# Hymba block on one core: unit-matrix transposes in TensorE's first waits, a transfer counted in two halves, one rounding step moved

## The chip, the core and the metric

The kernel runs on one core of a Trainium2 chip. The core has a matrix engine (TensorE, in the profile PE, with its weight loads as PEld), a vector engine (VectorE, DVE), a scalar engine (ScalarE, ACT), GpSimd (POOL) and a queue processor (SyncE, SP) that only issues transfers here. Each engine works through its own instructions in program order, and the engines wait for each other on semaphores. The metric is the device time of one execution in microseconds, as the median over several executions.

## What is computed

One layer of a transformer-like block on x of 512 tokens by 2048 columns, all in float32:

```python
mod = (silu(c) @ w_ada + b_ada)            # six rows of 2048: shift, scale and gate for each sub-layer
shift_m, scale_m, gate_m, shift_f, scale_f, gate_f = split(mod, 6)
h = rmsnorm(x, g_pre_mix) * (1.0 + scale_m) + shift_m
y = token_mixer(h, w_in, ...)              # h @ w_in, attention and gated linear attention heads, @ w_out
x = x + gate_m * rmsnorm(y, g_post_mix)
h = rmsnorm(x, g_pre_mlp) * (1.0 + scale_f) + shift_f
y = square(relu(h @ w_mlp_in)) @ w_mlp_out
x = x + gate_f * rmsnorm(y, g_post_mlp)
```

The change lies in the first stage alone: the normalised x, the row `scale_m`, and the first columns of `h @ w_in`.

## The kernel before

Every engine has one hand-written program, so the order of work on each engine is the order of its code.

The first stage runs like this. ACT squares and sums the four 128-token blocks of x, POOL forms the inverse roots, and DVE and ACT scale two blocks each (`scale_x`). TensorE then transposes x, 16 column tiles k of four 128x128 transposes each, into six PSUM banks in turn, and ACT copies each tile out (`xn_t`). One transpose is a matmul instruction against the unit matrix `ident`.

Beside this DVE works on `scale_m`. The 2048 by 2048 piece of `w_ada` comes in 16 items `am_item` of four 128x512 slabs, four items to a block of 512 columns, and each item comes as two transfers of two slabs. `add_am(n)` multiplies the slabs of item n by the column of silu(c) and adds them into `am_acc` and `am_odd`; at a block's end the two are added. `sum_columns(block)` on TensorE then sums over the partitions with four matmuls against a column of ones, and `mod_columns(block)` on DVE turns that into the scale `mod_a` of four tiles k and raises `am_col`. `add_am` of the next block stands behind this in DVE's program.

With the scale of block 0 known, ACT forms `in_tmp` for k = 0 to 3 (`fill_operand`), and TensorE begins the "fill": the narrow gate columns (`wm_raw`) and the query columns (`fill_w`) of `h @ w_in`, four tiles k to a block. Half of the fill is done in plain float32 (even units u), half with operands split into a high and a low part (units 1, 3, 5, 7), three matmuls for one product (`split_mm`). For these, ACT rounds the weights (`fill_w_hi`, tile `fill_hi`) and the operand (`fill_x_hi`), and DVE forms the low parts (`fill_weights_lo` and `fill_pair_lo`). DVE's program around the first block, unchanged by the diff except inside `add_am`:

```python
add_items(0, 4)
mod_columns(0)
fill_weights_lo(1)      # waits for ACT's fill_hi of unit 1
add_items(4, 6)
fill_pair_lo(1)
add_items(6, 8)
mod_columns(1)          # waits for TensorE's sum_columns(1)
```

TensorE's program for the fill calls `sum_columns(1)` inside unit 1, ahead of its tile k = 3, so TensorE can't go past this place before DVE has finished `add_items(6, 8)`.

Semaphores named in the change: `am_in[3]` counts the transfers of slot 3, `out_done` those of the output at the very end.

Of the kernel before, what the change touches and what calls it, by code (L numbers as in the profile page):

```python
# [41 lines left out]
P = 128  # L42
# [3 lines left out]
def build_block(nc, x, c, w_ada, b_ada, g_pre_mix, g_post_mix, w_in, b_fgate, w_gla_a2, b_gla_a2,  # L46
                g_fox_out, g_gla_out, w_out, g_pre_mlp, g_post_mlp, w_mlp_in, w_mlp_out, out):
    _, SEQ, D = x.shape
    KT = D // P
    TB = SEQ // P  # L50
# [63 lines left out]
    with ExitStack() as ctx:  # L114
# [95 lines left out]
        def small(name, shape, dt=F32):  # L210
            t = at(name, shape, k_at[0], dt)
            size = 4
            for n in shape[1:]:
                size *= n
            k_at[0] += (size + 31) // 32 * 32
            return t

        ident = small("ident", [P, P])
# [34 lines left out]
        BA, BB = bank[6], bank[7]  # L253
# [6 lines left out]
        def sem(name):  # L260
            return ctx.enter_context(nc.semaphore(name))
# [8 lines left out]
        am_in = [sem(f"am_in{s}") for s in range(4)]  # L270
# [7 lines left out]
        out_done = sem("out_done")  # L278
# [182 lines left out]
        def hid_arrived(o):  # L461
            q = hid_at[o]
            return hop_in[q], 32 * (hid_uses[q].index(o) + 1)
# [23 lines left out]
        PIECES += [(slice(0, SEQ), k) for k in range(KT // 2, KT)]  # L487
        N_PIECES, SECOND, N_SECOND = len(PIECES), KT // 2, KT

        def items_used(n):  # L490
            return AM_BLOCK * (n // 4) + 4 * (n % 4)

# [2 lines left out]
        def gates_read(block):  # L495
            return 3 * block + 1

        def fill_read(u):
            return gates_read(u // 2) + 1 + u % 2 if u < MM_G - 1 else FILL_TILE + GLA_HEADS - 1

        FILL_TILE = gates_read(S_BLOCKS - 1) + 2
        gg_hi_done, GG_HI = fill_halves, 3 * len(SPLIT_UNITS) + 1
        gg_lo_done, GG_LO = fill_w_lo, len(SPLIT_UNITS) + 1
        ada_split, ADA_SPLIT = fill_x_lo, 2 * len(SPLIT_UNITS) + GLA_HEADS
# [23 lines left out]
        block = ctx.enter_context(nc.Block())  # L528
# [3 lines left out]
        def _(sp):  # L532
# [111 lines left out]
            def load_am(n):  # L644
                if n >= 4:
                    sp.wait_ge(am_used, items_used(n - 3))
                block, i = divmod(n, 4)
                col = (SCALE_M, SHIFT_M)[block // S_BLOCKS] + block % S_BLOCKS * 512
                for half in range(2):
                    k = 4 * i + 2 * half  # L650
                    sp.dma_start(am_item[n % 4][:, 2 * half:2 * half + 2, :], w_ada_t[:, k:k + 2, col:col + 512])\
                        .then_inc(am_in[n % 4], 16)

            def load_x(t):
                sp.dma_start(x_raw[:, t, :], x_t[:, t, :]).then_inc(x_in[t], 16)
# [12 lines left out]
            for block in range(S_BLOCKS):  # L668
                for n in range(4 * block, 4 * block + 4):
                    load_am(n)  # L670
                load_wm(block)
                for u in (2 * block, 2 * block + 1):
                    load_fill(u)
# [3 lines left out]
            for n in range(16, 32):  # L677
                load_am(n)
                for mm in FOX_AFTER.get(n, ()):
                    load_fox(0, mm, wait=mm > 1)  # L680
# [83 lines left out]
            for u in range(UNITS):  # L764
                n = 7 * u
# [44 lines left out]
            for half in range(2):  # L810
                sp.wait_ge(o_ready, 3 + half)
                sp.dma_start(out_t[:, 1, half * D // 2:(half + 1) * D // 2], v_raw[raw_at[UNITS][ROLE_OF_T[1]]][:, half, :])\
                    .then_inc(out_done, 16)
            sp.wait_ge(out_done, 16 * (TB + 1))


        @block.tensor
        def _(pe):
# [172 lines left out]
            pe.wait_ge(rows_in, 16 * 9)  # L991
            pe.transpose(bank[5][:, 0:6 * KT], rows_a[:, :], ident[0:6 * KT, 0:6 * KT])
            pe.transpose(bank[5][:, 128:148], rows_b[:, :], ident[0:20, 0:20]).then_inc(rows_steps, 1)
            for k in range(KT):
                if k == 0:
                    pe.wait_ge(xn_ready, TB)
                    pe.wait_ge(rows_steps, COLS_READY)
                if k >= TILES:
                    pe.wait_ge(xt_act, k - TILES + 1)
                for t in range(TB):  # L1000
                    last = pe.transpose(bank[k % TILES][:, t * P:t * P + P], x_raw[:, t, k * P:k * P + P], ident[:, :])
                last.then_inc(x_tr, 1)

            def sum_columns(block):
                pe.wait_ge(am_used, items_used(4 * block + 4))
                if block:
                    pe.wait_ge(am_col, block)
                for j in range(4):
                    col = block // S_BLOCKS * 4 + j
                    last = pe.matmul(BA[:, col:col + 1], am_acc[block % 3][:, j * P:j * P + P], ones[:, 0:1],  # L1010
                                     start=True, stop=True)
                last.then_inc(am_sum, 1)

            sum_columns(0)
            pe.wait_ge(xt_act, KT)
            FILL_SUMS = {3: 1, 7: 2, 11: 3, 14: S_BLOCKS}

# [190 lines left out]
            for i, (n, h) in enumerate(halves):  # L1208
                u, p = n // 7, n % 7
                _, dc, group = unit_at[u]  # L1210
                first = u == 0 or unit_at[u - 1][2] != group
                o = 7 * group + p
# [5 lines left out]
                if u and first and h == 0:  # L1218
                    done, count = hid_arrived(o)
# [44 lines left out]
        def _(act):  # L1264
# [150 lines left out]
            def fill_operand(k):  # L1415
                act.wait_ge(am_col, k // 4 + 1)
                act.activation(in_tmp[:, k, :], xn_t[:, k, :], ACT.Copy, scale=mod_a[:, k:k + 1]).then_inc(fill_tmp, 1)
# [14 lines left out]
            def park(h):  # L1432
                act.wait_ge(fill_used, FILL_TILE + h)
                act.activation(gg[:, h * 512:h * 512 + 512], bank[h][:, :], ACT.Copy).then_inc(fill_park, 1)

            def fill_w_hi(u):
                i = SPLIT_UNITS.index(u)
                act.wait_ge(fill_in[u // 2], 64)
                if i > 1:
                    act.wait_ge(fill_used, fill_read(SPLIT_UNITS[i - 2]))  # L1440
                act.activation(fill_hi[i % 2][:, :, :, :], fill_w[u][:, :, :, :], ACT.Copy).then_inc(fill_halves, 1)

            def fill_x_hi(k):
                act.wait_ge(fill_tmp, k + 1)
                act.activation(in_hi[:, k, :], in_tmp[:, k, :], ACT.Copy).then_inc(fill_halves, 1)

            for block in range(S_BLOCKS):
                units = [u for u in SPLIT_UNITS if u // 2 == block]
                fill_w_hi(units[0])
                for k in range(4 * block, 4 * block + 4):  # L1450
                    fill_operand(k)
                for u in units:
                    if u != units[0]:
                        fill_w_hi(u)
                    fill_x_hi(2 * u)
                    fill_x_hi(2 * u + 1)
# [252 lines left out]
            t, cg, done, count = SQUARES[-1]  # L1709
# [34 lines left out]
        def _(dve):  # L1744
# [272 lines left out]
            def add_am(n):  # L2017
                block, i = divmod(n, 4)
                total = am_acc[block % 3]
                dve.wait_ge(am_in[n % 4], 32 * (n // 4 + 1))  # L2020
                if i == 0 and block >= 3:
                    dve.wait_ge(am_sum, block - 2)
                for j in range(4):
                    part = (total, am_odd)[j % 2][:, :]
                    item, c_k = am_item[n % 4][:, j, :], c_act[:, 4 * i + j:4 * i + j + 1]
                    if i or j > 1 or (j and block):
                        dve.wait_ge(am_used, items_used(n) + j - 1)
                    if i or j > 1:
                        dve.scalar_tensor_tensor(part, item, c_k, part, ALU.mult, ALU.add).then_inc(am_used, 1)
                    else:  # L2030
                        dve.tensor_scalar(part, item, c_k, None, ALU.mult).then_inc(am_used, 1)
                if i == 3:
                    dve.wait_ge(am_used, items_used(n) + 4)
                    dve.tensor_tensor(total[:, :], total[:, :], am_odd[:, :], ALU.add).then_inc(am_used, 1)
# [55 lines left out]
            def add_items(first, end):  # L2090
                for n in range(first, end):
                    add_am(n)
# [14 lines left out]
            fill_weights_lo(3)  # L2107
            fill_pair_lo(3)
            add_am(11)
            mod_columns(2)  # L2110
            add_items(12, 14)
            fill_weights_lo(5)
            add_items(14, 16)
            fill_pair_lo(5)
            fill_weights_lo(7)
            add_am(16)
            mod_columns(3)
            add_items(17, 20)
# [333 lines left out]
            for i in range(len(halves)):  # L2452
# [24 lines left out]
                u = i // 14  # L2477
# [192 lines left out]
```

## Time and profile before

| | before |
|---|---|
| median of 3 executions | 2203.49 us (2203.16 to 2205.0) |
| the profiled execution, its own time | 2203.36 us |
| span of its instructions | 2201.6 us |
| mean granted TensorE clock | 0.998 |
| TensorE busy | 2161.7 us, 98% of the span |
| VectorE busy | 1542.9 us, 70% |
| ScalarE busy | 883.0 us, 40% |
| GpSimd busy | 377.8 us, 17% |

The span is the time from the first to the last instruction of the core; the execution's own time is 1.8 us longer. Times in the rows are microseconds from the span's start. A matmul's recorded duration is longer than the distance to the next one, because matmuls overlap; so start times are compared, not durations. A float32 matmul against moving data is recorded as two passes, and a transpose as one.

### The profile page before, as it was taken

The page shows a single profiled execution, that of the slowest core. Times are in us where ns is not written, and L with a number is a line of the kernel's source. Part 1 is how long each engine was busy: PE and PEld are TensorE (multiplying, and loading weights), DVE is VectorE, ACT ScalarE, POOL GpSimd, SP SyncE. Part 2 cuts the span into 40 slices and gives each one's busy share as a digit, 9 for nine tenths or more (in the row PEclk, how much of TensorE's full clock was granted, in tenths as well). Part 3 has the DMA queues.
Part 4 walks back from the last instruction along what each step waited for, and adds up shares of the span by engine and source line. Part 5 has one row for each costly group of instructions (what it writes and reads, how often), then busy time and mean ns, then how long its engine had stood idle before and what let it go on. Part 6 is the DMA issues. An engine that isn't in the chain of part 4 may idle for free.

```text
span 2201.6 us, 26767 instructions
## 1 busy us (share of the span) xinstructions
PE 2161.7 (98%) x9821; PEld 1756.6 (80%) x9821; DVE 1542.9 (70%) x1604; ACT 883.0 (40%) x1129; POOL 377.8 (17%) x210
## 2 busy tenths in 40 slices
PE   6999999999999999999999999999999999999998
PEld 3688888887777887888888888888788888888886
DVE  6887667677886625744454465445789898898988
ACT  5353333332343224543533434435444444444443
POOL 1000000000000001000000000000036454454645
PEclk9999999999999999999999999999999999999999
DMA  9966657655544345464675666655374666567673
GB/s 362 341 228 228 207 169 237 198 172 165 160 148 140 138 172 171 169 222 166 205 254 182 206 205 230 205 185 184 125 250 149 240 214 203 173 239 242 232 237 143
DMA packets 258469, 445.46 MB, mean 202 GB/s; under 512 B 18284, under 2 KB 102576, under 8 KB 252344
## 3 DMA queue, kind: packets, MB, share of 16 engines
q1 hardware_dynamic: 257536, 439.71, 59.5%
q10 hardware_dynamic: 824, 4.27, 0.5%
q8 instruction: 71, 1.16, 0.2%
q14 instruction: 38, 0.31, 0.0%
HBM read 384.14 MB, written 59.79 MB: 202 GB/s over the span
## 4 chain that ended last, share of the span: by engine, by line
PE 85%; issue 8%; DVE 3%; ACT 1%; POOL 1%; DMA 1%; DVEq 1%; POOLq 0%; SPq 0%; ACTq 0%
PE pair L821 26%; PE pair L823 26%; PE pair L822 26%; PE pair L1033 1%; DVE v_op L2372 1%; PE pair L922 1%; PE pair L896 1%; PE pair L1044 1%; DMA x_raw<-in_x 1%; POOL v_sum L2619 0%; PE pair L913 0%; PE pair L962 0%; DVE y_t L2422 0%; PE pair L863 0%; PE pair L971 0%
## 5 line engine op out<-in xcount | busy, mean ns | idle before, releaser
L821 PE MATMUL pair<-in_hi,w_hi 128*128 128x512 f32 (+1 forms) x1760 | 700.1, 398 | 3.9 <-DVE in_lo L2275 3.8
L823 PE MATMUL pair<-in_hi,w_lo 128*128 128x512 f32 (+1 forms) x1760 | 680.7, 387 | 0.0
L822 PE MATMUL pair<-in_lo,w_hi 128*128 128x512 f32 (+1 forms) x1760 | 679.7, 386 | 0.0
L1749 DVE TENSOR_TENSOR w_lo<-w_raw,w_hi 128x2048 fp32r<-128x2048 f32 (+2 forms) x142 | 286.3, 2016 | 363.2 <-ACT w_hi L1269 362.7
L1269 ACT ACTIVATE w_hi<-w_raw 128x2048 fp32r<-128x2048 f32 (+2 forms) x142 | 238.4, 1679 | 412.6 <-PE pair L823 404.6
L821 PEld LDWEIGHTS pair<-in_hi,w_hi 128*128 128x128 f32 x1760 | 331.2, 188 | 76.3 <-issue 9.9
L823 PEld LDWEIGHTS pair<-in_hi,w_lo 128*128 128x128 f32 x1760 | 330.9, 188 | 68.4
L822 PEld LDWEIGHTS pair<-in_lo,w_hi 128*128 128x128 f32 x1760 | 331.5, 188 | 64.9 <-issue 1.9
L821 PE MATMUL pair<-v_op,hid_r 128*128 128x512 f32 x896 | 349.1, 390 | 2.2 <-issue 0.8
L823 PE MATMUL pair<-v_op,hid_r 128*128 128x512 f32 x896 | 348.7, 389 | 0.0
L822 PE MATMUL pair<-v_op,hid_r 128*128 128x512 f32 x896 | 348.6, 389 | 0.0
L2372 DVE TENSOR_TENSOR v_op<-v_raw,v_op 128x1024 fp32r<-128x1024 f32 x192 | 302.3, 1595 | 65.4 <-ACT v_op L1722 64.3
L1722 ACT ACTIVATE v_op<-v_raw 128x1024 fp32r<-128x1024 f32 x192 | 203.3, 1061 | 287.6 <-PE pair L823 269.2
L2619 POOL TENSOR_TENSOR v_sum<-v_raw,v_raw 128x512 f32<-128x512 f32 x60 | 149.2, 2514 | 363.4 <-DVE v_raw L2387 363.4
L821 PEld LDWEIGHTS pair<-v_op,hid_r 128*128 128x128 f32 x896 | 168.2, 188 | 39.2 <-issue 3.6
L823 PEld LDWEIGHTS pair<-v_op,hid_r 128*128 128x128 f32 x896 | 168.2, 188 | 35.1
L822 PEld LDWEIGHTS pair<-v_op,hid_r 128*128 128x128 f32 x896 | 168.2, 188 | 34.6
L2628 POOL TENSOR_TENSOR v_raw<-v_raw,v_sum 128x512 f32<-128x512 f32 x60 | 135.3, 2286 | 18.4 <-DVE v_op L2372 18.4
L2543 POOL TENSOR_TENSOR ada<-ada,c_act 128x2048 f32<-128x2048 f32 x8 | 32.3, 4039 | 588.8 <-DMA ada<-in_w_ada 551.5
L2422 DVE TENSOR_TENSOR y_t<-pair,y_t 128x1024 f32<-128x1024 f32 x104 | 124.9, 1214 | 0.3 <-PE pair L823 0.3
L821 PE MATMUL pair<-w_hi,in_hi 128*128 128x512 f32 x256 | 100.8, 394 | 0.3 <-issue 0.3
L822 PE MATMUL pair<-w_lo,in_hi 128*128 128x512 f32 x256 | 99.7, 389 | 0.0
(257 smaller groups left out, 2047.7 us busy)
## 6 DMA issues: line engine op xcount, KB each, us to landing
w_raw<-in_w_mlp_in SPq DMA_DIRECT2D x64, 1024.0 KB, 5.4
v_raw<-in_w_mlp_out SPq DMA_DIRECT2D x128, 512.0 KB, 5.0
hid_r<-hid_scratch SPq DMA_DIRECT2D x112, 512.0 KB, 6.5
hid_scratch<-hid_r SPq DMA_DIRECT2D x28, 1792.0 KB, 6.6
am_item<-in_w_ada SPq DMA_DIRECT2D x64, 512.0 KB, 8.7
af_item<-in_w_ada SPq DMA_DIRECT2D x64, 512.0 KB, 4.7
w_raw<-in_w_in SPq DMA_DIRECT2D x96, 256.0 KB, 3.4
w_raw<-in_w_in SPq DMA_DIRECT2D x160, 128.0 KB, 3.3
```

Source lines behind the costliest of these rows:

```text
L821: pe.matmul(dst, a[0], b[0], start=start, stop=False, skip_group_check=onto)
L822: pe.matmul(dst, a[0], b[1], start=False, stop=False, skip_group_check=onto)
L823: return pe.matmul(dst, a[1], b[0], start=False, stop=stop, skip_group_check=onto)
L896: pe.matmul(BA[:, 0:(i + 1) * P], grp[:, q_tile, i * P:i * P + P], grp[:, k_tile, 0:(i + 1) * P], start=True, stop=True).then_inc(fox_qk, 1)
L1269: act.activation(view(w_hi[n]), view(w_raw[n]), ACT.Copy).then_inc(hi_done, 1)
L1722: act.activation(v_op[i % 4][:, 0, :], raw_of(u, p)[:, h, :], ACT.Copy).then_inc(v_hi, 1)
L1749: dve.tensor_tensor(view(w_lo[n]), view(w_raw[n]), view(w_hi[n]).bitcast(F32), ALU.subtract)\
L2372: dve.tensor_tensor(v_op[i % 4][:, 1, :], raw_of(u, p)[:, h, :], v_op[i % 4][:, 0, :].bitcast(F32), ALU.subtract).then_inc(v_lo, 1)
L2422: return dve.tensor_tensor(dst, src[:, :, :], dst, ALU.add)
L2543: pool.tensor_tensor(unit[:, :, :], unit[:, :, :], c_act[:, :].rearrange("p (k o) -> p k o", o=1).to_broadcast([P, KT, P]), ALU.mult)\
L2619: last = pool.tensor_tensor(v_sum[:, h, cols], v_raw[q[B22]][:, h, cols], v_raw[q[B11]][:, h, cols], ALU.add)
L2628: last = pool.tensor_tensor(b21, b21, v_sum[:, h, cols], ALU.subtract)
```

## The change

It has three parts.

- TensorE gets a helper `keep_clock(n, bank)`, which transposes the unit matrix n times into a PSUM bank that nobody reads: 38 times ahead of the transposes of x, 10 times ahead of `sum_columns(0)`, and 13 times behind it.
- The second transfer of item 3 (the last of block 0) counts on a semaphore of its own, so that DVE can begin on the item's first two slabs when these are there, and waits again ahead of the third. The semaphore is `out_done`, whose last count is raised to match.
- In block 0 alone, ACT forms the four `in_tmp` before `fill_hi` of unit 1, and not after it.

```diff
--- before.py
+++ after.py
@@ -487,6 +487,8 @@
         PIECES += [(slice(0, SEQ), k) for k in range(KT // 2, KT)]
         N_PIECES, SECOND, N_SECOND = len(PIECES), KT // 2, KT
 
+        WARM_X, WARM_SUM, WARM_FILL = 38, 10, 13
+
         def items_used(n):
             return AM_BLOCK * (n // 4) + 4 * (n % 4)
 
@@ -499,6 +501,7 @@
             return gates_read(u // 2) + 1 + u % 2 if u < MM_G - 1 else FILL_TILE + GLA_HEADS - 1
 
         FILL_TILE = gates_read(S_BLOCKS - 1) + 2
+        am_tail, OUT_DONE = out_done, 16 + 16 * (TB + 1)
         gg_hi_done, GG_HI = fill_halves, 3 * len(SPLIT_UNITS) + 1
         gg_lo_done, GG_LO = fill_w_lo, len(SPLIT_UNITS) + 1
         ada_split, ADA_SPLIT = fill_x_lo, 2 * len(SPLIT_UNITS) + GLA_HEADS
@@ -648,8 +651,9 @@
                 col = (SCALE_M, SHIFT_M)[block // S_BLOCKS] + block % S_BLOCKS * 512
                 for half in range(2):
                     k = 4 * i + 2 * half
+                    done = am_tail if n == 3 and half else am_in[n % 4]
                     sp.dma_start(am_item[n % 4][:, 2 * half:2 * half + 2, :], w_ada_t[:, k:k + 2, col:col + 512])\
-                        .then_inc(am_in[n % 4], 16)
+                        .then_inc(done, 16)
 
             def load_x(t):
                 sp.dma_start(x_raw[:, t, :], x_t[:, t, :]).then_inc(x_in[t], 16)
@@ -811,7 +815,7 @@
                 sp.wait_ge(o_ready, 3 + half)
                 sp.dma_start(out_t[:, 1, half * D // 2:(half + 1) * D // 2], v_raw[raw_at[UNITS][ROLE_OF_T[1]]][:, half, :])\
                     .then_inc(out_done, 16)
-            sp.wait_ge(out_done, 16 * (TB + 1))
+            sp.wait_ge(out_done, OUT_DONE)
 
 
         @block.tensor
@@ -991,6 +995,11 @@
             pe.wait_ge(rows_in, 16 * 9)
             pe.transpose(bank[5][:, 0:6 * KT], rows_a[:, :], ident[0:6 * KT, 0:6 * KT])
             pe.transpose(bank[5][:, 128:148], rows_b[:, :], ident[0:20, 0:20]).then_inc(rows_steps, 1)
+            def keep_clock(n, unread):
+                for _ in range(n):
+                    pe.transpose(unread[:, 0:P], ident[:, :], ident[:, :])
+
+            keep_clock(WARM_X, BA)
             for k in range(KT):
                 if k == 0:
                     pe.wait_ge(xn_ready, TB)
@@ -1011,7 +1020,9 @@
                                      start=True, stop=True)
                 last.then_inc(am_sum, 1)
 
+            keep_clock(WARM_SUM, BA)
             sum_columns(0)
+            keep_clock(WARM_FILL, BB)
             pe.wait_ge(xt_act, KT)
             FILL_SUMS = {3: 1, 7: 2, 11: 3, 14: S_BLOCKS}
 
@@ -1446,11 +1457,12 @@
 
             for block in range(S_BLOCKS):
                 units = [u for u in SPLIT_UNITS if u // 2 == block]
-                fill_w_hi(units[0])
+                if block:
+                    fill_w_hi(units[0])
                 for k in range(4 * block, 4 * block + 4):
                     fill_operand(k)
                 for u in units:
-                    if u != units[0]:
+                    if block == 0 or u != units[0]:
                         fill_w_hi(u)
                     fill_x_hi(2 * u)
                     fill_x_hi(2 * u + 1)
@@ -2017,11 +2029,13 @@
             def add_am(n):
                 block, i = divmod(n, 4)
                 total = am_acc[block % 3]
-                dve.wait_ge(am_in[n % 4], 32 * (n // 4 + 1))
+                dve.wait_ge(am_in[n % 4], 32 * (n // 4 + 1) - (16 if n % 4 == 3 else 0))
                 if i == 0 and block >= 3:
                     dve.wait_ge(am_sum, block - 2)
                 for j in range(4):
                     part = (total, am_odd)[j % 2][:, :]
+                    if n == 3 and j == 2:
+                        dve.wait_ge(am_tail, 16)
                     item, c_k = am_item[n % 4][:, j, :], c_act[:, 4 * i + j:4 * i + j + 1]
                     if i or j > 1 or (j and block):
                         dve.wait_ge(am_used, items_used(n) + j - 1)
```

ACT's program in the first blocks, before. `x_raw` to `xn_t` is the transposed x, and the numbers behind tile names tell buffers apart.

```order
14 L1413 ACTIVATE xn_t<-pair 128x512 [waits x_tr] x16
15 L1441 ACTIVATE fill_hi_98<-fill_w_91 128x1024 [waits fill_in0]
16 L1417 ACTIVATE in_tmp<-xn_t,mod_a 128x512 [waits am_col] x4
17 L1445 ACTIVATE in_hi<-in_tmp 128x512 [waits fill_tmp] x2
18 L1441 ACTIVATE fill_hi_99<-fill_w_93 128x1024 [waits fill_in1]
```

The same place in ACT's program with the change.

```order
14 L1424 ACTIVATE xn_t<-pair 128x512 [waits x_tr] x16
15 L1428 ACTIVATE in_tmp<-xn_t,mod_a 128x512 [waits am_col] x4
16 L1452 ACTIVATE fill_hi_98<-fill_w_91 128x1024 [waits fill_in0]
17 L1456 ACTIVATE in_hi<-in_tmp 128x512 [waits fill_tmp] x2
18 L1452 ACTIVATE fill_hi_99<-fill_w_93 128x1024 [waits fill_in1]
```

`fill_hi` of the first block now stands behind the four `in_tmp`, which wait for `am_col`. In the second block the order is as before.

DVE's program with the change, from the third slab of item 3 on. The rows are those of before but for the added wait on `out_done`.

```order
23 L2043 SCALAR_TENSOR_TENSOR am_acc_86<-am_item_85,c_act,am_acc_86 128x512 [waits am_used,out_done]
24 L2043 SCALAR_TENSOR_TENSOR am_odd<-am_item_85,c_act,am_odd 128x512 [waits am_used]
25 L2048 TENSOR_TENSOR am_acc_86<-am_acc_86,am_odd 128x512 [waits am_used]
26 L2098 TENSOR_TENSOR mod_a<-pair,cols_a 128x4 [waits am_sum]
27 L2100 TENSOR_TENSOR mod_a<-mod_a,cols_a 128x4
28 L2071 TENSOR_TENSOR fill_lo_101<-fill_w_91,fill_hi_98 128x1024 [waits fill_halves]
29 L2045 TENSOR_SCALAR am_acc_87<-am_item_82,c_act 128x512 [waits am_in0]
```

`fill_lo` did not move: it still stands ahead of the first instruction of block 1's items, and it waits (on `fill_halves`) for the `fill_hi` that moved on ACT.

TensorE's program with the change around the first sum; the two rows of `pair<-ident` are new.

```order
26 L1010 MATMUL pair<-ident,x_raw 128x128 x3
27 L1000 MATMUL pair<-ident 128x128 x10
28 L1019 MATMUL pair<-ones,am_acc_86 128x1 [waits am_used]
29 L1019 MATMUL pair<-ones,am_acc_86 128x1 x3
30 L1000 MATMUL pair<-ident 128x128 x13
31 L1055 MATMUL pair<-in_tmp,wm_raw 40x512 [waits fill_tmp,fill_in0,xt_act]
```

The 10 stand between the transposes of x and the sum, the 13 between the sum and the fill. A third new row, of 38, stands ahead of the first transpose of x.

## Rows read from the trace of the kernel before

**Rows 1.** The page: its first line, and TensorE's busy time.

```profile
span 2201.6 us, 26767 instructions
...
PE 2161.7 (98%) x9821; PEld 1756.6 (80%) x9821; DVE 1542.9 (70%) x1604; ACT 883.0 (40%) x1129; POOL 377.8 (17%) x210
```

**Rows 2.** Timeline of TensorE, first 75 us: start, duration, instruction, idle before.

```profile
11.21 0.29 PE L993 MATMUL pair<-ident,rows_b 20*128 20x20 f32 x1
19.73 9.38 PE L1001 MATMUL pair<-ident,x_raw 128*128 128x128 f32 x64 [8.23 <-ACT x_raw L1402]
28.95 0.95 PE L1010 MATMUL pair<-ones,am_acc 128*128 128x1 f32 x8
31.95 3.60 PE L1044 MATMUL pair<-in_tmp,wm_raw 128*40 128x512 f32 x8 [2.05 <-ACT in_tmp L1417]
...
45.22 0.95 PE L1010 MATMUL pair<-ones,am_acc 128*128 128x1 f32 x8
...
62.26 0.95 PE L1010 MATMUL pair<-ones,am_acc 128*128 128x1 f32 x8
```

**Rows 3.** Timeline of ScalarE, first 120 us.

```profile
20.89 0.60 ACT L1413 ACTIVATE xn_t<-pair 128x512 f32<-128x512 f32 x1 [1.21 <-PE pair L1001]
...
24.30 5.98 ACT L1413 ACTIVATE xn_t<-pair 128x512 f32<-128x512 f32 x12 [0.26 <-PE pair L1001]
30.04 1.18 ACT L1441 ACTIVATE fill_hi<-fill_w 128x1024 fp32r<-128x1024 f32 x1
30.99 2.64 ACT L1417 ACTIVATE in_tmp<-xn_t,mod_a 128x512 f32<-128x512 f32 x4
33.44 1.22 ACT L1445 ACTIVATE in_hi<-in_tmp 128x512 fp32r<-128x512 f32 x2
...
46.64 2.56 ACT L1417 ACTIVATE in_tmp<-xn_t,mod_a 128x512 f32<-128x512 f32 x4 [3.29 <-DVE mod_a L2086]
```

**Rows 4.** Timeline of VectorE, first 120 us.

```profile
24.91 0.75 DVE L2029 SCALAR_TENSOR_TENSOR am_acc<-am_item,c_act,am_acc 128x512 f32<-128x512 f32 x1 [0.21 <-DMA am_item<-in_w_ada]
...
27.68 0.69 DVE L2034 TENSOR_TENSOR am_acc<-am_acc,am_odd 128x512 f32<-128x512 f32 x1
...
30.17 0.16 DVE L2086 TENSOR_TENSOR mod_a<-mod_a,cols_a 128x4 f32<-128x4 f32 x1
31.25 1.23 DVE L2057 TENSOR_TENSOR fill_lo<-fill_w,fill_hi 128x1024 fp32r<-128x1024 f32 x1 [0.91 <-ACT fill_hi L1441]
...
43.78 0.69 DVE L2034 TENSOR_TENSOR am_acc<-am_acc,am_odd 128x512 f32<-128x512 f32 x1
...
46.45 0.16 DVE L2086 TENSOR_TENSOR mod_a<-mod_a,cols_a 128x4 f32<-128x4 f32 x1
...
59.23 0.69 DVE L2034 TENSOR_TENSOR am_acc<-am_acc,am_odd 128x512 f32<-128x512 f32 x1
```

**Rows 5.** Windows of 1 us: busy and count per engine, PEclk, DMA share, GB/s.

```profile
22.00:23.00 1.00, 1.00 (x7) 1.00 (x6) 1.00 (x2) 0.74 (x2) 0.00 (x0) 1.00 1.07 391
...
26.00:27.00 1.00, 1.00 (x12) 1.00 (x11) 1.00 (x3) 1.00 (x3) 0.00 (x0) 1.00 1.04 383
```

**Rows 6.** The same view around a wait of TensorE in mid-kernel.

```profile
666.00:667.00 1.00, 0.13 (x1) 0.00 (x0) 0.93 (x3) 1.00 (x1) 0.00 (x0) 1.00 0.79 227
667.00:668.00 1.00, 0.07 (x1) 0.10 (x1) 0.97 (x3) 0.79 (x1) 0.00 (x0) 1.00 0.00 0
...
669.00:670.00 1.00, 1.00 (x5) 0.80 (x4) 0.93 (x2) 0.00 (x0) 0.00 (x0) 0.68 0.00 0
670.00:671.00 1.00, 1.00 (x4) 0.81 (x3) 1.00 (x2) 0.00 (x0) 0.00 (x0) 0.50 0.00 0
671.00:672.00 1.00, 1.00 (x4) 0.72 (x4) 1.00 (x1) 0.12 (x1) 0.00 (x0) 0.50 0.00 0
672.00:673.00 1.00, 1.00 (x4) 0.84 (x3) 0.56 (x1) 0.47 (x1) 0.00 (x0) 0.62 0.00 0
```

**Rows 7.** The line of `sum_columns`: its weight loads, duration in ns min/median/max.

```profile
L1010 PEld LDWEIGHTS pair<-ones,am_acc x64: 187/192/192, 28.8 to 147.5; 128*128 128x128 f32 x64
```

## The prediction

> **What bounds the kernel now.** I read the page first. TensorE is busy for 2161.7 of 2201.6 us [rows 1]. So a change to the first stage is worth what it shifts TensorE's work from there on, and nothing else. The reader is to look for the moment from which TensorE runs without a wait, and for what set that moment.
>
> The timeline of TensorE comes next [rows 2]. After two small transposes that end at 11.50 (11.21 + 0.29) it waits 8.23 us for the last block of scaled x. It transposes from 19.73, sums block 0 from 28.95, waits 2.05 us for ACT's `in_tmp`, and begins the fill at 31.95. The next sum, of block 1, starts at 45.22 without an idle time ahead of it.
>
> The timelines of ACT and DVE show what these waits hang on. ACT's first and fifth copy of transposed tiles start at 20.89 and 24.30 [rows 3]: four tiles of four transposes in 3.41 us, 0.213 us for each transpose. The other 44 of the 64 take from about 24.27 to 28.95 [rows 2], 0.106 us each. The windows show the same step, 7 starts in a microsecond and later 12 [rows 5]. That is the 1.2 GHz level and then the 2.4 GHz level, though the granted clock is given as 1.00 in both rows; in the first stage I go by the spacing. ACT's copies then run back to back to 30.28 (24.30 + 5.98), `fill_hi` follows at 30.04, `in_tmp` at 30.99 [rows 3], and TensorE at 31.95.
>
> DVE is the third strand. It ends block 0 at 28.37 (27.68 + 0.69), has `mod_a` ready behind its instruction of 30.17, waits 0.91 us for `fill_hi`, starts `fill_lo` at 31.25, and is then busy without a listed idle time until 44.47 (43.78 + 0.69), when block 1's total is ready [rows 4]. TensorE asks for it at 45.22 [rows 2]. So DVE has 0.75 us to spare there. This is the number on which my forecast turns. At block 2 the same two events are 59.92 and 62.26 [rows 2, 4], 2.34 us to spare.
>
> **The 38 transposes.** They can start at 11.50. All at 0.213 us they would take 8.1 us and end at 19.6, ahead of 19.73, so they can't delay the transposes of x. They read only `ident`, add no transfer and stand ahead of nothing else. If some 20 of them are slow, as the 20 transposes of x were, and 18 fast, they end at 11.5 + 4.3 + 1.9 = 17.7, and TensorE sits idle for 2.0 us. The idle time at 29.9 to 31.95 was 2.05 us long, and the fill's eight passes behind it took 3.60 us [rows 2], the faster level. So I take it that the clock is still up at 19.73. Then 64 transposes at 0.106 us end at 26.5, against 28.95. ACT's copies, 0.50 us each (5.98 / 12), begin after one tile and the same hand-over, at about 20.4, and end at 28.4, against 30.28.
>
> A rule to weigh here stands in the Trainium skill, "TensorE: Matmul & The Clock Gate", Part 4: PE-mode transpose. It says that the full clock does not engage for transposes, because they don't count as busy in the same way. By that rule the 38 buy nothing. The trace disagrees: it is transposes alone that run when their spacing falls from 0.213 to 0.106 us, and a stretch of 64 slow ones would have ended at 19.73 + 13.6 = 33.4, not 28.95.
>
> **The split transfer.** DVE waited 0.21 us for item 3 [rows 4]. With the first half counted alone that wait can go; at best the whole 0.21, at worst nothing. I take 0.21: block 0 ends at 28.16. The first matmul of the sum needs a weight load first, 0.19 us [rows 7], and some hand-over; I take 0.25 together, estimated, so the sum starts at 28.41. The 10 transposes end at 26.5 + 1.1 = 27.6, ahead of it.
>
> **The scale.** Before, from the sum's first matmul at 28.95 to `mod_a`'s second instruction at 30.17 is 1.22 us [rows 2, 4]; from that instruction to ACT's first `in_tmp` is 0.19 us in the block where ACT stands ready (46.45 to 46.64) [rows 3, 4]. So the first `in_tmp` starts at 28.41 + 1.22 + 0.19 = 29.82. ACT is free by 28.4. From the end of the ACT instruction ahead (30.04 + 1.18 = 31.22) to TensorE's start at 31.95 was 0.73 us, so the fill now can start at 29.82 + 0.73 = 30.55, which is 1.40 us earlier. The 13 transposes end at 28.41 + 0.8 + 13 x 0.106 = 30.6: they cost about nothing, and 1.4 us more if the clock were down.
>
> **The moved rounding step.** It makes room for this, and it is what DVE pays for. `fill_hi` now starts when four `in_tmp` are issued, 2.45 us (30.99 to 33.44) after the first: 29.82 + 2.45 = 32.27. DVE's `fill_lo` started 1.21 us after `fill_hi` did (30.04 to 31.25) [rows 3, 4], so it now starts at 33.48 and not at 31.25. That is 2.23 us later, and behind it in DVE's queue stand all of block 1's items. DVE had no idle time between 31.25 and 44.47 in which to catch up, so block 1's total comes at 44.47 + 2.23 = 46.70. TensorE would be at its second sum at 45.22 - 1.40 = 43.82. It now waits there, and its first matmul starts at 46.70 + 0.25 = 46.95. Against 45.22 that is **1.73 us later** than before. The gain of 1.40 us is spent in this wait.
>
> Behind it the two engines keep their distance. DVE's next step, `mod_a`, waits for this very sum, so block 2's total moves by the same 1.73 us as TensorE does, and its 2.34 us to spare stay. DMA's items are issued when DVE frees their slots, at most 2.23 us later, 0.5 us more than the rest; that is inside the 2.34. The rest of the kernel moves as a whole.
>
> **What the new wait does to the clock.** It lasts from 43.82 to about 46.75, 2.9 us. In mid-kernel TensorE had 1.80 us idle (0.87 + 0.93), and at 669.3 the granted clock fell to 0.50 for some 3.3 us; the lost share is 0.32 + 0.50 + 0.50 + 0.38 = 1.70 us [rows 6]. The idle 2.05 us at 30 to 32 cost nothing. A wait of 2.9 us is longer than both, so a fall is likelier than not. Its price is between nothing and 1.70 us, less where the slow stretch lies partly in the wait itself. I take 1.0.
>
> **Sum.** 2203.36 (the profiled execution) + 1.73 + 1.0 = 2206.1 us. The profiled execution is 0.13 us under the median of 2203.49, which I neglect. The parts without price: `keep_clock` writes banks nobody reads, and the raised last count at the end waits for the same transfers as before. I call a change within 0.2%, 4.4 us here, no change that a measurement of this kernel can tell.
>
> **Rivals.**
>
> *The gain is kept.* If block 1's total were in time, the kernel would end 1.40 us earlier: 2202.0. DVE would have to make up 2.23 + 1.40 - 0.5 = 3.1 us before the sum, and its rows show nothing to make it up from. For it speaks only that this is one execution and that my hand-overs are short distances read from few rows. Chance 0.12. A case close to it, in which most of the lateness is hidden and the time stays within 1 us of before (2202.5 to 2204.5), gets 0.08.
>
> *The unit-matrix transposes don't hold the clock up*, the slower side. Then the transposes of x end as before, the 10 are added behind them, and the sum starts at 28.95 + 1.06 = 30.0. `in_tmp` starts at 31.4, `fill_lo` at 31.4 + 2.45 + 1.21 = 35.1, which is 3.8 us late; block 1's total comes at 48.3 and the sum at 48.55, 3.3 us later than before. With 0 to 1.70 us for a fall in the wait: 2206.7 to 2208.4. This turns to "slower" (over 2207.9) only if nearly the whole fall is paid on top. For it speaks a 2.0 us idle time behind the 38, longer than the 1.80 us of rows 6. Chance 0.13. The Trainium skill's rule on transposes would lead here.
>
> *More than one late strand.* If one more wait of TensorE in blocks 2 to 5 appears because the transfers come later than I take, some 2 to 3 us are added and the time is 2208 to 2210. Chance 0.07.
>
> **How the numbers follow.** The forecast itself, TensorE 1.73 us late and 0 to 1.70 us for the clock, spans 2205.1 to 2206.8 and has 0.60. The range of 2202.0 to 2208.4 takes in all cases but the last. Faster by over 0.2% would need 4.4 us, which no case gives; I leave 0.03. Slower by over 0.2% gets the last case and the top of the clock rival, 0.10. Within 0.2%: 0.87.
>
> **What the changed kernel's profile would show.** Right: transposes of x from 19.73 take under 7 us; the fill starts at about 30.5; ACT's `fill_hi` starts near 32.3, behind the four `in_tmp`; DVE idles some 3 us ahead of `fill_lo`; and TensorE waits 2.5 to 3 us for DVE ahead of the second sum, which starts near 47. Wrong: if the second sum starts before 45.2, my count of DVE's slack is wrong and the gain stands. If the transposes of x still take 9 us, the clock rival holds. If the fall of the clock shows in rows behind 47, its price is read there.

## The result and the profile after

The changed kernel takes 2207.05 us (median of 20 executions, 2204.19 to 2208.78), the kernel before 2203.51 us in as many. The ratio is 1.0014, 95% interval 1.0009 to 1.002. So the change costs some 3.5 us. That is inside the 0.2% that I called no change, but its interval excludes 1.

The page of the changed kernel, first line and busy times.

```profile
span 2206.7 us, 26890 instructions
...
PE 2171.5 (98%) x9882; PEld 1764.4 (80%) x9882; DVE 1542.6 (70%) x1604; ACT 882.7 (40%) x1129; POOL 376.8 (17%) x210
```

The 61 added matmuls are there (9882 against 9821) [rows 1], and the span is 5.1 us longer. This profiled execution took 2208.53 us, at the top of its range. Timeline of TensorE in it.

```profile
11.38 5.72 PE L1000 MATMUL pair<-ident 128*128 128x128 f32 x38
19.70 8.87 PE L1010 MATMUL pair<-ident,x_raw 128*128 128x128 f32 x64 [2.60 <-ACT x_raw L1413]
28.41 1.25 PE L1000 MATMUL pair<-ident 128*128 128x128 f32 x10
29.50 0.95 PE L1019 MATMUL pair<-ones,am_acc 128*128 128x1 f32 x8
30.31 1.62 PE L1000 MATMUL pair<-ident 128*128 128x128 f32 x13
31.86 3.63 PE L1055 MATMUL pair<-in_tmp,wm_raw 128*40 128x512 f32 x8
...
47.73 1.36 PE L1019 MATMUL pair<-ones,am_acc 128*128 128x1 f32 x8 [2.44 <-DVE am_acc L2048]
...
68.03 0.95 PE L1019 MATMUL pair<-ones,am_acc 128*128 128x1 f32 x8
```

Two things stand against rows 2. The second sum, which TensorE reached without an idle time before, is now behind a wait of 2.44 us for DVE, and starts 2.51 us later (47.73 against 45.22). In this execution the gain ahead of it never came: the transposes of x took 8.87 us, and the fill starts at 31.86 against 31.95. So 1.2 us of the 2.51 belong to the start of this one execution (see "The changed kernel once more", where the second sum starts at 46.53). And between the second and the third sum, where nothing was changed, 20.30 us pass where 17.04 did; the third is 5.77 us later.

Timeline of VectorE, the same execution.

```profile
30.73 0.16 DVE L2100 TENSOR_TENSOR mod_a<-mod_a,cols_a 128x4 f32<-128x4 f32 x1
34.46 1.23 DVE L2071 TENSOR_TENSOR fill_lo<-fill_w,fill_hi 128x1024 fp32r<-128x1024 f32 x1 [3.57 <-ACT fill_hi L1452]
...
46.99 0.69 DVE L2048 TENSOR_TENSOR am_acc<-am_acc,am_odd 128x512 f32<-128x512 f32 x1
```

`fill_lo` starts 3.21 us later than in rows 4, and the total of block 1 comes 3.21 us later too: nothing between them gave any of it back.

Windows of 1 us: busy time and count of PE, PEld, DVE, ACT and POOL, then granted clock, DMA share and GB/s.

```profile
20.00:21.00 1.00, 1.00 (x12) 1.00 (x11) 1.00 (x2) 0.61 (x2) 0.00 (x0) 1.00 1.04 385
21.00:22.00 1.00, 1.00 (x8) 1.00 (x6) 1.00 (x3) 0.97 (x2) 0.00 (x0) 0.51 1.06 387
22.00:23.00 1.00, 1.00 (x6) 1.00 (x5) 1.00 (x2) 0.60 (x1) 0.00 (x0) 0.50 1.04 381
...
24.00:25.00 1.00, 1.00 (x9) 1.00 (x8) 1.00 (x3) 0.83 (x2) 0.00 (x0) 0.79 1.26 229
...
47.00:48.00 1.00, 0.27 (x3) 0.27 (x3) 0.68 (x1) 0.00 (x0) 0.00 (x0) 1.00 1.03 381
48.00:49.00 1.00, 1.00 (x9) 1.00 (x8) 0.00 (x0) 0.00 (x0) 0.00 (x0) 0.66 1.06 391
49.00:50.00 1.00, 1.00 (x4) 0.81 (x5) 0.79 (x4) 0.43 (x1) 0.00 (x0) 0.50 1.05 371
...
55.00:56.00 1.00, 1.00 (x3) 0.23 (x2) 1.00 (x2) 0.00 (x0) 0.00 (x0) 0.93 1.05 391
```

The granted clock falls to 0.50, the 1.2 GHz level, twice. Behind the idle 2.60 us ahead of the transposes of x it is low from 21 to 24.4: 0.49 + 0.50 + 0.50 + 0.21 = 1.70 us lost. Behind the new wait it is low from 48.3 to 55.1: 0.34 + 6 x 0.50 + 0.07 = 3.41 us lost. In return the fall at 669.3 of rows 6 is missing in this execution: the same wait of TensorE comes (1.81 us idle until 674.53), and the granted clock behind it stays at 1.00.

### The profile page after: what moved, and what is told of

Its sections match the earlier page's. It is cut to its first block, busy times and chain, and to the rows that moved or that the text cites. A ratio compares the mean times of both kernels' runs of the same rounds, so it can differ in the third digit from the quotient of the medians.

```text
span 2206.7 us, 26890 instructions
## 1 busy us (share of the span) xinstructions
PE 2171.5 (98%) x9882; PEld 1764.4 (80%) x9882; DVE 1542.6 (70%) x1604; ACT 882.7 (40%) x1129; POOL 376.8 (17%) x210
## 4 chain that ended last, share of the span: by engine, by line
PE 84%; issue 8%; DVE 4%; DMA 1%; POOL 1%; ACT 1%; DVEq 1%; SPq 0%; POOLq 0%; ACTq 0%
PE pair L825 26%; PE pair L827 26%; PE pair L826 26%; PE pair L1044 1%; DVE v_op L2386 1%; PE pair L926 1%; PE pair L900 1%; DMA x_raw<-in_x 1%; PE pair L1055 1%; POOL v_sum L2633 0%; PE pair L1010 0%; PE pair L917 0%; DMA w_raw<-in_w_in 0%; PE pair L966 0%; DVE y_t L2436 0%
```

## Experiments

Each set of kernels was timed beside the kernel before, whose medians in the three sets were 2203.14, 2203.30 and 2203.26 us.

### The rounding step put back

`no_move` is the changed kernel with ACT's old order in block 0:

```diff
-                if block:
-                    fill_w_hi(units[0])
+                fill_w_hi(units[0])
                 for k in range(4 * block, 4 * block + 4):
                     fill_operand(k)
                 for u in units:
-                    if block == 0 or u != units[0]:
+                    if u != units[0]:
                         fill_w_hi(u)
```

> The changed kernel with the rounding step of block 0 back at its old place ahead of the four in_tmp; the unit-matrix transposes and the split transfer stay. Theory (the moved step makes VectorE late): fill_lo starts between 30.7 and 32.0, VectorE's total of block 1 is ready at 43.9 to 45.2, TensorE has no wait over 0.3 us there, the granted clock stays up between 45 and 55, and the time is 2202.5 to 2203.7, some 3 to 4 us under the changed kernel. Rival (the unit-matrix transposes do the harm, by way of the clock): the time stays at 2206 or more.

Measured: 2201.99 us (2201.32 to 2203.43, 11 executions), ratio 0.9994 (0.9985 to 1.0003). The same kernel once more, in another set:

> The version with the rounding step back in its old place (transposes and split transfer kept), once more, to see whether its gain repeats. Theory: 2201.5 to 2203.0, 0.5 to 1.5 us under the kernel before of this set; second sum at 44.6. If the first gain was chance, the time is that of before within 0.3 us.

2202.21 us (2201.85 to 2204.36), ratio 0.9996 (0.9987 to 1.0006). Both together have a median of 2202.1, which is 4.6 us under the repeated changed kernel (2206.66, below). Timeline of TensorE in the first:

```profile
30.63 3.63 PE L1055 MATMUL pair<-in_tmp,wm_raw 128*40 128x512 f32 x8
...
44.62 1.05 PE L1019 MATMUL pair<-ones,am_acc 128*128 128x1 f32 x8 [0.53 <-DVE am_acc L2047]
...
61.74 0.95 PE L1019 MATMUL pair<-ones,am_acc 128*128 128x1 f32 x8
```

And of VectorE, the same execution:

```profile
29.57 1.22 DVE L2070 TENSOR_TENSOR fill_lo<-fill_w,fill_hi 128x1024 fp32r<-128x1024 f32 x1
31.87 0.49 DVE L2044 TENSOR_SCALAR am_acc<-am_item,c_act 128x512 f32<-128x512 f32 x1 [1.08 <-DMA am_item<-in_w_ada]
```

The cause held. The time is 0.5 us under the range expected, `fill_lo` starts sooner (29.57), and TensorE still waits 0.53 us at the second sum. The early fill (30.63) doesn't need the move: ACT does `fill_hi` at 28.10, while it would wait for `mod_a` anyway. The second row of VectorE shows something that the trace of before hid: with `fill_lo` done early, DVE waits for item 4's transfer, until 31.87.

The lead doesn't last, though. At the second sum TensorE is 0.60 us ahead of the trace of before (44.62 against 45.22). Some 145 us later it transposes the tile `prob`, which ACT forms behind a step of DVE. Timeline of TensorE before:

```profile
189.76 0.41 PE L913 MATMUL pair<-ident,prob 128*128 128x128 f32 x2
```

And in `no_move`:

```profile
190.00 0.41 PE L917 MATMUL pair<-ident,prob 128*128 128x128 f32 x2 [0.72 <-ACT prob L1340]
```

Here TensorE waits 0.72 us and is 0.24 us behind the trace of before. `step_back_again` has a wait of 0.71 us at the same place, the changed kernel one of 0.72 us (to 196.39) and of 0.43 us in its second profile. What holds DVE and ACT there was not looked into.

### The move alone

`move_only` is the kernel before with only ACT's new order.

> The kernel before with the moved rounding step alone. Theory: in_tmp starts near 30.4 and the fill near 31.2, but fill_lo only at 34.1, VectorE's total of block 1 at 47.3, TensorE waits some 3 us ahead of its second sum and the clock falls behind it; the second sum is 2.3 us later than before, and with 1 to 3.4 us for the clock the time is 2206 to 2209. Rival (the transposes do the harm): within 1 us of before, 2203.5.

Measured: 2204.53 us (2203.77 to 2206.77), ratio 1.0008 (0.9999 to 1.0017): about 1.4 us slower by the medians, less than the 2206 to 2209 expected, and the interval just takes in no change. Timeline of TensorE in it:

```profile
31.74 5.29 PE L1044 MATMUL pair<-in_tmp,wm_raw 128*40 128x512 f32 x8 [1.34 <-ACT in_tmp L1417]
...
47.68 1.05 PE L1010 MATMUL pair<-ones,am_acc 128*128 128x1 f32 x8 [0.82 <-DVE am_acc L2035]
```

DVE's wait for `fill_hi` is 3.57 us again and the second sum is 2.46 us late (47.68 against 45.22). The wait there is only 0.82 us, since a fall of the clock in the fill (5.29 us for its first eight passes, 3.60 in rows 2) made TensorE late by itself. Where both strands are late, their delays overlap, and behind this short wait no further fall followed. The forecast had a wait of 3 us and the fall of the clock there, and this is where it missed.

### The clock held through the wait

`hold_stall` is the changed kernel with 26 more transposes of the unit matrix in the new wait. They take the place of idle time and change nothing else in the order.

```diff
+                    if k == 3:
+                        keep_clock(26, bank[4])
                     if k in FILL_SUMS:
                         sum_columns(FILL_SUMS[k])
```

> The changed kernel with 26 more unit-matrix transposes, into a free bank, ahead of the second sum, so that TensorE is busy in the wait for VectorE. Theory: the sum is as late as in the changed kernel (within 0.4 us), but the clock stays up behind it; the profile's second sum to third sum takes 17.0 us as before and not 20.3, and the time is 2204 to 2206. If the late sum itself were harmless and only the clock cost, the time would come back to 2203.5; if the clock cost nothing, it would stay at 2207.

Measured: 2204.23 us (2203.39 to 2205.04), ratio 1.0004 (0.9995 to 1.0013). Timeline of TensorE:

```profile
30.60 3.63 PE L1057 MATMUL pair<-in_tmp,wm_raw 128*40 128x512 f32 x8
...
43.89 3.00 PE L1000 MATMUL pair<-ident 128*128 128x128 f32 x26
46.72 0.95 PE L1019 MATMUL pair<-ones,am_acc 128*128 128x1 f32 x8
...
63.74 0.95 PE L1019 MATMUL pair<-ones,am_acc 128*128 128x1 f32 x8
```

The lateness of the second sum stays (46.72), and the third follows 17.02 us later, the 17.04 of before. No fall of the clock follows the wait, and the fall at 669.3 is missing in this profile too.

### The changed kernel once more

> The changed kernel once more, beside the other runs of this set. Theory (late sum 1.5 us, plus a fall of the clock in the wait for it in most executions, plus a fall ahead of the transposes of x in some): 2205.5 to 2207.5, the executions spread over more than 3 us. If the late sum alone counted, it would be 2204.5 with a narrow spread, as with the wait filled (2204.23).

Measured: 2206.66 us (2205.12 to 2209.33), ratio 1.0015 (1.0006 to 1.0024). In this profiled execution TensorE idled 2.02 us ahead of the transposes of x, the clock stayed up, and they took 7.21 us. Timeline of TensorE behind that:

```profile
46.53 1.86 PE L1019 MATMUL pair<-ones,am_acc 128*128 128x1 f32 x8 [2.45 <-DVE am_acc L2048]
...
66.70 0.95 PE L1019 MATMUL pair<-ones,am_acc 128*128 128x1 f32 x8
```

Windows of the same execution, columns as above:

```profile
46.00:47.00 1.00, 0.47 (x3) 0.47 (x3) 0.47 (x1) 0.00 (x0) 0.00 (x0) 0.61 1.06 385
47.00:48.00 1.00, 1.00 (x6) 1.00 (x7) 0.00 (x0) 0.00 (x0) 0.00 (x0) 0.50 1.04 385
...
53.00:54.00 1.00, 1.00 (x4) 0.27 (x3) 1.00 (x2) 0.00 (x0) 0.00 (x0) 0.98 0.99 329
```

The fall behind the wait is the same size as in the other execution: 0.39 + 6 x 0.50 + 0.02 = 3.41 us lost. From the second sum to the third it is 20.17 us against the 17.02 of `hold_stall`, so 3.15 us were paid; the medians of the two differ by 2.43 us. The two kernels were timed in different sets, and the intervals of their ratios overlap, but the slowest of the 11 executions of `hold_stall` (2205.04 us) is under the fastest of these 11 (2205.12).

### DVE's low part behind item 5

`dve_later` swaps two calls in DVE's program of the changed kernel:

```diff
-            fill_weights_lo(1)
             add_items(4, 6)
+            fill_weights_lo(1)
```

> The changed kernel with VectorE's fill_weights_lo(1) moved behind its items 4 and 5. Theory (what costs is that block 1's items stand behind fill_lo, which waits for the moved step): VectorE no longer idles 3.6 us, its total of block 1 is ready at 43.0 to 44.1, TensorE does not wait at the second sum, and the time is 2202.1 to 2203.5. Rival (transposes and clock, or a later strand): 2206 or more.

Measured: 2205.10 us (2203.25 to 2206.62), ratio 1.0007 (0.9998 to 1.0016). By the medians it gave back 1.6 us of the changed kernel's 2206.66, and neither the 2202.1 to 2203.5 expected nor the wait of nothing at the second sum came true. The timeline of VectorE says why:

```profile
32.09 0.48 DVE L2045 TENSOR_SCALAR am_acc<-am_item,c_act 128x512 f32<-128x512 f32 x1 [2.26 <-DMA am_item<-in_w_ada]
34.82 0.75 DVE L2043 SCALAR_TENSOR_TENSOR am_acc<-am_item,c_act,am_acc 128x512 f32<-128x512 f32 x1 [0.52 <-DMA am_item<-in_w_ada]
```

The wait for `fill_hi` is gone, and 2.26 us for item 4 stand in its place. The total of block 1 came at 45.23 + 0.69 = 45.92, and TensorE's wait was 1.73 us, with a clock loss of 1.71 us behind it. That is only 0.50 us ahead of the total in `hold_stall` (46.42): `fill_lo`, 1.22 us long, now runs behind item 5, where `no_move` does it inside the wait for item 4 and has its total at 44.56.

### Item 4 asked for earlier

Then let the transfer come earlier. `item4_first` is `no_move` with item 4 queued ahead of the first gate and fill weights:

```diff
                 for n in range(4 * block, 4 * block + 4):
-                    load_am(n)
+                    if n != 4:
+                        load_am(n)
+                if block == 0:
+                    load_am(4)
                 load_wm(block)
```

> The changed kernel with the rounding step back in its old place, and the transfer of item 4 issued ahead of the loads of wm_raw and fill_w of block 0. Theory (with the step back, VectorE waits 1.08 us for item 4 and this is what is late next): that wait goes, the total of block 1 is ready 1 us earlier (near 43.5), the second sum has no wait and starts near 44.1, and the time is 0.5 us under the one with the step back, 2201.0 to 2202.0. Rival: the loads of wm_raw and fill_w now come 1.4 us later and the fill or fill_hi waits for them, the fill starts at 31.5 or later and the time is 2202.5 to 2203.5.

Measured: 2205.64 us (2203.91 to 2208.93), ratio 1.001 (1.0001 to 1.0019): slower than both the expectation and its rival. The weights behind it come late. Timeline of ScalarE:

```profile
32.08 1.06 ACT L1455 ACTIVATE fill_hi<-fill_w 128x1024 fp32r<-128x1024 f32 x1 [3.51 <-DMA fill_w<-in_w_in]
```

And of TensorE:

```profile
33.89 6.56 PE L1058 MATMUL pair<-in_tmp,wm_raw 128*40 128x512 f32 x8 [3.04 <-ACT in_tmp L1431]
```

In every window from 28 to 38 us the queues move 377 to 391 GB/s, so an item ahead is a weight behind. The rival had this, with a fill at 31.5 or later; it didn't have the clock, which is low from 33.0 to 39.9 behind the wait of 3.04 us (3.41 us lost). The profiled execution is the slowest of the 11.

### The unit-matrix transposes and the split transfer

`x_only` is the kernel before with the 38 alone, `dummies_only` with all three groups (38, 10, 13), `split_only` with the split transfer alone, and `no_move_x50` is `no_move` with `WARM_X` at 50.

> The kernel before with the 38 unit-matrix transposes ahead of x alone: not the 10 and 13, not the split transfer, not the moved step. Theory (the 38 are what gains, by the transposes of x ending at 26.6 to 27): the first sum near 28.6, the fill near 30.8, VectorE's total of block 1 near 44.1 because the transfer of item 4 holds it, the second sum near 44.6 and the time 2202.0 to 2203.0. If the 10 and 13 are needed to hold the clock, it falls in the waits between 26.6 and 30.8 and the time is 2204 or more.

Measured: 2203.50 us (2202.11 to 2204.21), ratio 1.0003 (0.9994 to 1.0012). The transposes of x took 7.21 us, but the timeline of TensorE goes on like this:

```profile
28.61 1.05 PE L1015 MATMUL pair<-ones,am_acc 128*128 128x1 f32 x8 [1.62 <-DVE am_acc L2039]
31.00 6.27 PE L1049 MATMUL pair<-in_tmp,wm_raw 128*40 128x512 f32 x8 [1.34 <-ACT in_tmp L1422]
```

The waits are now on both sides of the sum, the clock is low from 29.5 to 36.4 (3.42 us lost), and the gain is gone.

> The same without the split transfer: the kernel before with the 38, 10 and 13 unit-matrix transposes alone. Theory: with the transposes of x done at 27, VectorE's total of block 0 sets the first sum, so it now starts 0.4 us later than with the split (near 28.6) and the fill near 31.0; but item 4 of block 1 still comes at 31.9 and holds VectorE, so the second sum stays at 44.6 to 44.9 and the time is that of the version with the split within 0.5 us (2201.8 to 2203.3).

Measured: 2202.11 us (2201.29 to 2203.56), ratio 0.9996 (0.9986 to 1.0005). The fill starts at 31.12 and takes 3.63 us for its first eight passes. So the 10 and the 13 together keep what the 38 win at the fill. That is read from the traces; of the times, the medians differ by 1.39 us, but the intervals overlap. Which of the two groups is needed was not tried.

> The kernel before with the split transfer alone. Theory: VectorE's block 0 ends some 0.3 us earlier (28.1), but the sum still starts at 28.95 behind the transposes of x, so the time is that of before within 1 us (2202.2 to 2204.2). If VectorE's total set the sum, the fill would start 0.3 us earlier, which is too little to see in the time but not in the profile.

Measured: 2203.44 us (2201.65 to 2205.30), ratio 1.0004 (0.9995 to 1.0013). Block 0's total came at 28.06 (27.37 + 0.69), and the sum at 28.96, behind the slow transposes of x: no effect alone. With the transposes the fill starts 0.49 us earlier by it (30.63 in `no_move`, 31.12 in `dummies_only`), but item 4 holds the second sum (44.62 and 44.82), and nothing is seen in the time (2202.11 without it, 2202.1 with it).

> The version with the rounding step back, and 50 and not 38 unit-matrix transposes ahead of x. Theory: the 50 end between 18.3 and 20.3 by when the clock rises; where it rises late they hold the transposes of x up by at most 0.5 us, otherwise nothing changes but the idle time ahead of x (1.3 us down to about 0.3), so 2201.8 to 2203.3. If falls of the clock ahead of x were frequent with 38, the median would drop by over 0.5 us against the version with 38.

Measured: 2203.05 us (2201.91 to 2205.04), ratio 1.0 (0.999 to 1.0009). In its profiled execution the 50 took only 7.08 us (10.70 to 17.78), less than the 7.21 of the 38 in `dummies_only`. TensorE idled 2.33 us, the clock was low from 20.4 to 23.9, and the transposes of x took 8.87 us. So more of them didn't mean a shorter idle time in this execution: they began 0.9 us earlier than in `no_move` (11.64), and by the spacing (an estimate) some 17 of them were slow against 26 there. The median is 0.9 us above that of `no_move`, where half a microsecond below was expected if falls ahead of x were frequent with 38.

The best version of all is the changed kernel with the rounding step left at its old place: 2202.1 us, some 1.1 us (0.05%) under the kernel before by the medians, which these intervals can't tell from no change, and 4.6 us under the changed kernel, which they can. The traces don't show that this 1.1 us is the gain of the first stage, since that was gone at 190 us.

## Why the prediction came out as it did

**The mechanism was the one named.** The moved rounding step makes DVE wait for `fill_hi`, block 1's items stand behind it, and TensorE's second sum waits for their total. Undoing the move alone takes the loss away (`no_move`), and the move alone makes the second sum late (`move_only`), though it costs the time less. In `hold_stall`, where no fall of the clock disturbs the chain, the numbers of the text can be set against rows: the fill at 30.60 (30.55 foretold), `in_tmp` at 29.66 (29.82), `fill_hi` at 32.12 (32.27), `fill_lo` at 33.20 (33.48), the total at 46.42 (46.70), the second sum at 46.72 (46.95). The sum is 1.50 us late, against the 1.73 forecast.

**The term that was mis-sized is the clock's.** I took 1.0 us between 0 and 1.70, the upper end from the one fall in the trace of before [rows 6]. Behind the new wait 3.41 us were lost in both profiled executions, twice that upper end: the low stretch lasted 6.8 us and not 3.4. Of this 3.15 us were paid between the second and the third sum. One row is no upper bound for a price. The median of 2207.05 us is above the 2205.1 to 2206.8 of the forecast proper and inside the wider range, whose upper part I had given to another rival.

**The rest didn't move as a whole.** "The rest of the kernel moves as a whole" held up to the third sum and no further. The table gives how late TensorE is against the trace of before, in us, at five places: the second sum, the third, the transposes of `prob` near 190, its first matmul behind the wait of rows 6 (667.93 before), and the end, by the profiled executions' own times.

| | 2nd sum | 3rd sum | 190 | 668 | end |
|---|---|---|---|---|---|
| changed, first profile | 2.51 | 5.77 | 6.63 | 6.60 | 5.17 |
| changed, `after_again` | 1.31 | 4.44 | 4.81 | 4.80 | 3.38 |
| `hold_stall` | 1.50 | 1.48 | 1.50 | 1.51 | 0.03 |
| `no_move` | -0.60 | -0.52 | 0.24 | 0.18 | 0.07 |
| `step_back_again` | -0.44 | -0.35 | 0.68 | 0.61 | -0.86 |

My sum leaves out two things. The wait near 190 adds 0.4 to 1.0 us in four of the five. And the fall of the clock at 669, which the trace of before has, is missing in all but `no_move`; by the last two columns its absence is worth some 1.45 us. For the changed kernel the terms by `after_again` are 1.31 for the late sum, 3.13 for the clock, 0.36 for what follows and -1.42 for the missing fall: 3.38, against my 2.73. So a clock term that was too small by 2 us was in good part offset by a fall that didn't come, and that the forecast lies so close is partly luck. Between medians the late sum alone (`hold_stall`) costs 1.09 us, and its interval takes in no change.

**The 38 transposes.** That they bring the clock up held: their spacing falls from 0.213 to 0.106 us. The Trainium skill, "TensorE: Matmul & The Clock Gate", Part 4: PE-mode transpose, says that the full clock doesn't engage for transposes; the runs disagree, for in `no_move` 38 of them took 6.82 us and the 64 of x 7.21, where slow ones take 8.1 and 13.6. That the clock is still up at 19.73 held in eight of the ten profiled executions that had these transposes, with idle times of 1.26 to 2.04 us. In the first one of the changed kernel (2.60 us) and in `no_move_x50` (2.33 us) it fell; the transposes then took 8.87 us and the sum came at 29.50 where it was 28.19 in `after_again`. This is the clock rival, in a milder form (the sum at 29.50 and not 30.0) and in some executions only.

**The split transfer and the 13.** I counted 0.21 us for the one and nothing for the other. The total of block 0 came at 28.08 in `hold_stall` (27.39 + 0.69), where I had 28.16; the split shows no effect on the time. The 13 cost next to nothing: from the first `in_tmp` to the fill are 0.94 us with them (`hold_stall`) and 0.87 without (`x_only`). Without them and the 10 the clock falls at 29.5 (`x_only`).

**DVE's slack.** "Its rows show nothing to make it up from" held, but my picture of the wait did not. Of the 3.57 us that DVE idles ahead of `fill_lo`, the move is not the only cause: item 4 isn't there before 31.9 to 32.1, and the total didn't come before 44.47 in any profile, whatever ACT did (44.56 in `no_move`). My rival "The gain is kept" needed it some 0.9 us sooner. In the kernel before, `fill_lo` ended at 32.48 (31.25 + 1.23) [rows 4] and hid this. This is also why `no_move` still waits 0.53 us at the second sum.

**Still open.** Why one wait of 2.44 us was followed by a low stretch of 6.8 us, and one of 1.80 us [rows 6] by one of 3.4 us, the runs don't say. Nor do they say why the fall at 669 comes in some executions only: `no_move` and `step_back_again` are the same kernel, the first profile has it and the second hasn't. So the median of a kernel depends on how often it comes. In the second set 11 of the 33 executions of the kernel before took 2201.0 to 2201.9 us and the others 2202.5 or more, which fits a fall that is missing in a third of them; the profiled execution of `split_only` (2201.65 us) is one without it. Whether the unit-matrix transposes or the move make it rarer is not shown, and with that it stays open what the 1.1 us of `no_move` are.

## What to carry to other kernels

When a step is moved back on one engine, look at who waits for it and what stands behind that waiting instruction in its queue: here 1.4 us won on TensorE were paid with 2 us of lateness on DVE. A new wait of the matrix engine has two prices, its length and the clock behind it, and the second can be the larger; unread transposes of the unit matrix in the wait take the second away. Put such a filler only where the engine waits anyway, and before a wait is removed look for the transfer that would hold the same instruction next. Then follow a lead through the later stages: the 0.6 us that `no_move` had at the second sum were gone at 190 us, where it waits for another strand.

## What was not expected of the hardware

- A wait of 2.45 us was followed by 6.8 us at the 1.2 GHz level (46.2 to 53.0 in `after_again`, from inside the wait on); in `x_only` 6.8 us of it began between waits of 1.62 and 1.34 us. Behind single waits of 1.34 (`move_only`), 1.73 (`dve_later`), 1.80 (rows 6), 2.33 and 2.60 us it lasted 3.4 us.
- Whether a wait of about 2 us brings a fall differs. Idle 2.02 and 2.04 us ahead of the transposes of x were free, 2.33 and 2.60 us were not, and in mid-kernel the same wait of 1.8 us had a fall in some executions and none in others, even of the same kernel (`no_move` and `step_back_again`).
- At the kernel's start the granted clock is given as 1.00 while transposes start 0.213 us apart; their spacing shows the level there.
